# The blockwise inverse of a chunked RWKV-7 scan: two groups of heads in turn, a product on all four 64x64 tiles of TensorE, and other joins

## The reference

```python
def step(S, inp):
    r_t, w_t, k_t, v_t, kk_t, b_t = inp
    sa = jnp.einsum('bhvk,bhk->bhv', S, -kk_t)
    S = (S * w_t[:, :, None, :] + sa[..., None] * b_t[:, :, None, :]
         + v_t[..., None] * k_t[:, :, None, :])
    y_t = jnp.einsum('bhvk,bhk->bhv', S, r_t)
    return S, y_t
```

## Time and profile before

| | us |
|---|---|
| median of 3 runs | 1396.06 |
| lowest, highest | 1393.89, 1396.39 |
| the profiled execution | 1395.23 |
| its span | 1393.4 |
| chunk 0, levels and joins (span time) | 100.5 to 134.1 |
| chunk 1, levels and joins (span time) | 160.5 to 185.4 |

### The profile page before, as it was taken

The page is one execution under the profiler, slowest core; times in us unless marked ns, Lnnn a source line. Parts: engine busy times, 40 slices in busy tenths (PEclk is TensorE's granted clock), DMA queues, the critical chain, the costliest instruction groups (busy, mean ns, idle before and its releaser), DMA issues.

```text
span 1393.4 us, 23529 instructions
## 1 busy us (share of the span) xinstructions
PE 1363.5 (98%) x9838; PEld 1175.4 (84%) x9838; DVE 950.9 (68%) x1480; ACT 748.2 (54%) x1262; POOL 62.7 (5%) x63
## 2 busy tenths in 40 slices
PE   6999999999999999999999999999999999999998
PEld 6789888888889778888899877888888898788886
DVE  7896776766675776756667545576666697767565
ACT  6874435555456575545453446455545536555543
POOL 0003440000010000000000000000000000000000
PEclk9999999999999999999999999999999999999999
DMA  9411016555555315555565553545555553455551
GB/s 333 165 65 33 4 36 238 182 188 193 194 205 173 133 59 169 194 186 199 189 233 182 182 180 123 181 166 197 182 195 194 198 176 127 151 184 194 196 184 58
DMA packets 35290, 230.67 MB, mean 166 GB/s; under 512 B 4176, under 2 KB 5504, under 8 KB 8560
## 3 DMA queue, kind: packets, MB, share of 16 engines
q1 hardware_dynamic: 33376, 223.43, 46.4%
q0 software_dynamic: 1808, 5.74, 1.2%
HBM read 228.08 MB, written 1.05 MB: 164 GB/s over the span
## 4 chain that ended last, share of the span: by engine, by line
PE 91%; DVE 6%; ACT 2%; issue 0%; DMA 0%; SPq 0%; DVEq 0%; ACTq 0%
PE bank L1805 17%; PE bank L1806 17%; PE bank L1807 17%; PE bank L1930 17%; PE bank L1933 8%; PE bank L2197 3%; PE bank L1762 1%; DVE wlo L992 1%; PE bank L2003 1%; PE bank L2021 1%; PE bank L2037 1%; PE bank L2214 1%; PE bank L2375 0%; ACT arena L629 0%; PE bank L2376 0%
## 5 line engine op out<-in xcount | busy, mean ns | idle before, releaser
L992 DVE TENSOR_TENSOR wlo<-raw,whi 128x1024 fp32r<-128x1024 f32 (+1 forms) x416 | 492.9, 1204 | 249.9 <-ACT whi L454 245.5
L454 ACT ACTIVATE whi<-raw 128x1024 fp32r<-128x1024 f32 (+1 forms) x416 | 425.4, 1041 | 329.4 <-PE bank L1807 231.7
L1805 PE MATMUL bank<-whi,XHL 128*128 128x512 f32 x872 | 342.2, 392 | 0.0
L1806 PE MATMUL bank<-wlo,XHL 128*128 128x512 f32 x872 | 339.6, 389 | 0.0
L1807 PE MATMUL bank<-whi,XHL 128*128 128x512 f32 x872 | 339.5, 389 | 0.0
L1930 PE MATMUL bank<-XHL,whi 128*128 128x512 f32 x1008 | 316.6, 395 | 0.2
L1933 PEld LDWEIGHTS bank<-XHL,wlo 128*128 128x128 f32 x1008 | 189.3, 188 | 44.5
L1933 PE MATMUL bank<-XHL,wlo 128*128 128x256 f32 x1008 | 198.0, 278 | 0.0
L1805 PEld LDWEIGHTS bank<-whi,XHL 128*128 128x128 f32 x872 | 163.7, 188 | 34.2 <-issue 1.7
L1807 PEld LDWEIGHTS bank<-whi,XHL 128*128 128x128 f32 x872 | 163.7, 188 | 34.2
L1806 PEld LDWEIGHTS bank<-wlo,XHL 128*128 128x128 f32 x872 | 163.8, 188 | 32.7 <-issue 0.5
(11 more groups left out here) (302 smaller groups left out, 1265.0 us busy)
## 6 DMA issues: line engine op xcount, KB each, us to landing
raw<-in_w_mlp SPq DMA_DIRECT2D x128, 1024.0 KB, 4.9
raw<-in_w_rv SPq DMA_DIRECT2D x8, 1024.0 KB, 4.9
raw<-in_w_rg SPq DMA_DIRECT2D x8, 1024.0 KB, 5.0
raw<-in_w_reo SPq DMA_DIRECT2D x8, 1024.0 KB, 4.9
raw<-in_w_k SPq DMA_DIRECT2D x4, 1024.0 KB, 10.8
raw<-in_w_v SPq DMA_DIRECT2D x4, 1024.0 KB, 10.0
raw<-in_w_r SPq DMA_DIRECT2D x4, 1024.0 KB, 5.0
raw<-in_w_rwo SPq DMA_DIRECT2D x4, 1024.0 KB, 5.0
```

The lines of the kernel that those rows point to most:

```text
L454: act.activation(high, full, ACT.Copy).then_inc(hi_done, 1)
L992: dve.tensor_tensor(low, full, high, ALU.subtract).then_inc(lo_done, 1)
L1805: pe.matmul(out_, xh[xs], wh[ws], start=start, stop=False)
L1806: pe.matmul(out_, xh[xs], wl[ws], start=False, stop=False)
```

## The change

The heads are split in another way: two groups `q` of four columns, each with its even and odd heads. Buffers become `[p, q, f, h, s]`. Per level and group:

- `halves(c, i, q)`: the first product of four even and four odd heads. Even heads stay on the two tiles of before, odd heads write the other half of the partitions (`BLOCKS[blk ^ f]`), so all four tiles are used, in the order (0,0), (1,1), (0,1), (1,0).
- ScalarE copies the even heads (128 partitions, 256 wide) and, in two copies of 64 partitions, puts the odd heads' halves back in place.
- `inverse(c, i, q)`: the second product, as before on two tiles; it waits for the even copy, and then for the odd ones. VectorE subtracts and transposes by group.

The order on TensorE is `halves` of group 0, `inverse` of group 1 of the level before, `halves` of group 1, `inverse` of group 0.

The corner of even and odd heads shares one bank and one copy. The first join is made by group, on two tiles; the second comes behind the first pair products and (in chunk 0) the bonus sum, and the copies' waits move to the `sa` product of the first group. Four bonus products move from level 4 to level 2. `zero_tail` goes: the upper tokens of the `sa` product contract 64 rows instead of 128.

```diff
             def level(c, i, work):
 
-                for f in range(2):
-                    n = 10 * c + 2 * i + f
-                    rows = slice(0, P if i < 4 else HD)
+                rows = slice(0, P if i < 4 else HD)
+                for q in range(2):
+                    n = 10 * c + 2 * i + q
                     dve.wait_ge(inv_prod, n + 1)
-                    dve.tensor_tensor(TI_[rows, f], TI_[rows, f], bank8(6 + f)[rows], ALU.subtract).then_inc(inv_doubled, 1)
-                for f in range(2):
+                    ti = flat(TI_[rows, q])
+                    dve.tensor_tensor(ti, ti, psum[INVERSE_BANK[q]][rows, :], ALU.subtract).then_inc(inv_doubled, 1)
                     if i < 4:
-                        dve.wait_ge(inv_doubled, 10 * c + 2 * i + f + 1)
-                        dve.transpose(TT_[:, f], TI_[:, f]).then_inc(doubled, 1)
+                        dve.wait_ge(inv_doubled, n + 1)
+                        dve.transpose(flat(TT_[:, q]), flat(TI_[:, q])).then_inc(doubled, 1)
...
-                for i in range(5):
-                    for f in range(2):
-                        act.wait_ge(half_prod, 10 * c + 2 * i + f + 1)
-                        act.activation(PM[c][:, f], psum[4 + f][:, :].rearrange("p (h s) -> p h s", h=KT), ACT.Copy)\
-                            .then_inc(half_ready, 1)
+                for i in range(5):
+                    for q in range(2):
+                        even, odd = (psum[b][:, 0:T].rearrange("p (h s) -> p h s", h=4) for b in HALF_BANK[q])
+                        act.wait_ge(half_prod, 10 * c + 2 * i + q + 1)
+                        act.activation(PM[c][:, q, 0], even, ACT.Copy).then_inc(half_ready, 1)
+                        for to, source in ((TOP, LOW), (LOW, TOP)):
+                            act.activation(PM[c][to, q, 1], odd[source], ACT.Copy).then_inc(half_ready, 1)
...
-                if i == 4:
-                    dve.wait_ge(rho_ready, 2)
+                for q in {2: (0,), 4: (1,)}.get(i, ()):
+                    dve.wait_ge(rho_ready, q + 1)
...
-                    for p in range(KT):
+                    for p in range(4 * q, 4 * q + 4):
...
+            def halves(c, i, q):
+
+                keys = MBM[c][i % 2] if i else FIRST_KEYS[c]
+                if i == 0:
+                    pe.wait_ge(ti_ready, 2 * c + 2)
+                    pe.wait_ge(first_masked, 2 * c + 2)
+                    pe.wait_ge(corner_ready, c + 1)
+                    pe.wait_ge(beta_ready, 2 * c + 2)
...
+                else:
+                    pe.wait_ge(inv_doubled, 10 * c + 2 * (i - 1) + q + 1)
+                    pe.wait_ge(level_masked, 8 * c + 2 * (i - 1) + q + 1)
+                for h in range(4):
+                    for f in range(2):
+                        for blk in range(2):
+                            rows, o = BLOCKS[blk], BLOCKS[blk ^ f]
+                            ins = pe.matmul(psum[HALF_BANK[q][f]][o, h * HD:(h + 1) * HD], keys[rows, q, f, h],
+                                            TI_[rows, q, f, h], start=(h == 0), stop=(h == 3))
+                ins.then_inc(half_prod, 1)
+
+            def inverse(c, i, q):
+
+                for f in range(2):
+                    pe.wait_ge(half_ready, 30 * c + 6 * i + 3 * q + 2 * f + 1)
...
+                    ins = both(INVERSE_BANK[q], TT_, PM[c], q, f, 2 if i < 4 else 1)
+                ins.then_inc(inv_prod, 1)
+                if i == 4:
+                    for f in range(2):
+                        ins = both(STEP_BANK[q], PM[c], TT_, q, f)
+                    ins.then_inc(step_prod, 1)
+
+            def first_join(c, q):
+
+                pe.wait_ge(inv_doubled, 10 * c + 8 + q + 1)
+                pe.wait_ge(last_doubled, 2 * c + q + 1)
+                for h in range(4):
+                    p, cols = 4 * q + h, slice(h * HD, (h + 1) * HD)
+                    pe.matmul(psum[JOIN_BANK[q]][LOW, cols], CORNER[TOP, p], TI_[TOP, q, 0, h], start=(h == 0), stop=(h == 3))
+                    ins = pe.matmul(psum[JOIN_BANK[q]][TOP, cols], CORNER[LOW, p], TT_[LOW, q, 1, h], start=(h == 0),
+                                    stop=(h == 3))
+                ins.then_inc(p1_prod, 1)
+
+            def second_join(c):
+
+                pe.wait_ge(p1_ready, 2 * c + 2)
                 for p in range(KT):
...
+                    q, h, cols = p // 4, p % 4, slice(p * HD, (p + 1) * HD)
+                    for f, w, x in ((0, JOIN[LOW, p], TT_[LOW, q, 0, h]), (1, TI_[TOP, q, 1, h], JOIN[TOP, p])):
+                        ins = pe.matmul(psum[6 + f][TOP, cols], w, x, start=(p == 0), stop=(p == KT - 1))
...
                 for i in range(5):
...
+                    halves(c, i, 0)
                     if c == 0 and i < 4:
                         next(r_second)
+                    if i:
+                        inverse(c, i - 1, 1)
+                    halves(c, i, 1)
                     if c == 0 and i == 0:
                         next(r_second)
+                    inverse(c, i, 0)
+                inverse(c, 4, 1)
+                for q in range(2):
+                    first_join(c, q)
...
                 pair_products(c, 0)
...
+                second_join(c)
                 for g in range(4):
...
                     if g == 0:
-                        pe.wait_ge(tail_zeroed, c + 1)
+                        pe.wait_ge(t12_ready, 2 * c + 2)
+                        pe.wait_ge(t22_ready, 2 * c + 2)
                     for h in range(4):
                         p, f = 2 * g + h // 2, h % 2
-                        for t, w in zip(TOKEN_HALVES, (TT_, PM[c])):
-                            ins = pe.matmul(psum[4][t, 256 + h * HD:256 + (h + 1) * HD], w[:, f, p],
-                                            SR[g % 2][:, h * HD:(h + 1) * HD], start=(h == 0), stop=(h == 3))
+                        for t, rows, w in ((TOP, TOP, TT_), (LOW, slice(0, P), PM[c])):
+                            ins = pe.matmul(psum[4][t, 256 + h * HD:256 + (h + 1) * HD], w[rows, p // 4, f, p % 4],
+                                            SR[g % 2][rows, h * HD:(h + 1) * HD], start=(h == 0), stop=(h == 3))
```

More of the change, by code:

```diff
@@ L1714, in _ @@
             pool.wait_ge(gate_ready, 4)
-            zero_tail(1)
             pool.wait_ge(h_lo, 4 * MLP_STEPS)
@@ L2165, in corner @@
                         rows, ts, _ = half_tiles(c, f, 0)
-                        ins = pe.matmul(psum[4 * c + f][0:HD, p * HD:(p + 1) * HD], BE[rows, p, ts], AR[rows, 2 * p + c, 0, HD:P],
+                        be, kap = BE[rows, p, ts], AR[rows, 2 * p + c, 0, HD:P]
+                        ins = pe.matmul(psum[4 * c][rows, p * HD:(p + 1) * HD], kap if f else be, be if f else kap,
                                         start=(p == 0), stop=(p == KT - 1))
-                        if p == KT - 1:
-                            ins.then_inc(corner_prod, 1)
+                ins.then_inc(corner_prod, 1)
             def r_tiles():
@@ L2191, in _, with both @@
                 next(r_second)
-            def both(bank, w, x, f, blocks=2):
-                for p in range(KT):
-                    for blk in range(blocks):
-                        rows = slice(blk * HD, (blk + 1) * HD)
-                        ins = pe.matmul(psum[bank][rows, p * HD:(p + 1) * HD], w[rows, f, p], x[rows, f, p],
-                                        start=(p == 0), stop=(p == KT - 1))
-                return ins
+            BLOCKS = (TOP, LOW)
+            def both(bank, w, x, q, f, blocks=2):
+                for h in range(4):
+                    for blk in range(blocks):
+                        rows = BLOCKS[blk]
+                        ins = pe.matmul(psum[bank][rows, f * T + h * HD:f * T + (h + 1) * HD], w[rows, q, f, h],
+                                        x[rows, q, f, h], start=(h == 0 and f == 0), stop=(h == 3 and f == 1))
+                return ins
@@ L2244, in _ @@
                     if c == 0 and i < 4:
                         next(r_second)
-                    for f in range(2):
-                        n = 10 * c + 2 * i + f
-                        pe.wait_ge(half_ready, n + 1)
-                        if c and i == 0 and f == 0:
-                            pe.wait_ge(keys_ready, 4)
-                            pe.wait_ge(state_ready, 8)
-                        if i:
-                            pe.wait_ge(doubled, n - 1)
-                        else:
-                            pe.wait_ge(tt_ready, 2 * c + f + 1)
-                        both(6 + f, TT_, PM[c], f, 2 if i < 4 else 1).then_inc(inv_prod, 1)
-                        if i == 4:
-                            both(f, PM[c], TT_, f).then_inc(step_prod, 1)
+                    if i:
+                        inverse(c, i - 1, 1)
@@ L2314, in _ @@
                             pe.wait_ge(keys_ready, g)
+                        else:
+                            pe.wait_ge(t12_ready, 2)
                         for s, src in enumerate((BE, kT)):
@@ L2330, in _ @@
```

(2 more changed lines are left out.)

135 lines of the change are left out of this document (60 added, 75 removed).

## The result

The changed kernel takes 1413.18 us (1411.59 to 1413.69) against 1394.97 us for the kernel before, a ratio of 1.0129 with a 95% interval of 1.0117 to 1.0142. It is slower, as forecast. The forecast of 1410 was 3 us low: 1413.18 lies 0.2 us above its own range (1407 to 1413) and inside the wider one (1399.5 to 1416). The medians lie 18.2 us apart, where 14.5 was added up. The profiled execution took 1411.59 us with a span of 1409.8, that is 16.4 us more than the one of before, at the full granted clock (0.999 over the whole span); it was the fastest of the four, and the other three took 1.3 to 2.1 us more at granted clocks of 0.996 to 0.998.

What follows compares the result with a forecast made beforehand. TensorE, busy for 98% of the span, was taken as the bound. Terms 1.6 + 0.2 + 3.1 + 9.6 = 14.5 us gave 1410 us, own range 1407 to 1413, eight in ten 1399.5 to 1416.

Steps and rivals of the forecast that it cites:

- The gap: TensorE's wait for VectorE's subtraction between a group's second and next first product: priced at 1.0 us, about 0.8 shown idle.
- H: First product of an inverse level, 32 instructions per head group: on four tiles 0.51 us instead of 0.96.
- three pieces of the price: Wait at each half level: last matmul's start to VectorE 0.27, subtraction 0.69, VectorE's end to weight load 0.05; together 1.0 us.
- Chunk 0: First chunk's inverse, with a projection tile inside five levels that covers nothing: +3.1 us up to the bonus turn.
- Chunk 1: Second chunk's inverse and joins to the second pair products: +1.6 us, and +0.2 for VectorE's normalisation.
- H0(0): Group 0's first product at level 0 of the inverse, the zero from which chunk 1's times were counted.
- H0(1): Group 0's first product at level 1, put at 3.2 us in chunk 1, with the three copies overlapping.
- The mixed product: Product with the inverse, alternating 64-row and 128-row matmuls, eight times: seven shape changes, 1.2 us each product, +9.6 us.
- the upper bound: Mixed product's dearer end: each first weight load exposed by 0.05 us more, +1.4 us a product, 11.2 in all.
- No drain between the shapes: Rival for the mixed product: alternating shapes cost nothing, only the inverse's 4.9 us remain, 1401.0 us; chance 0.18.
- A stagger that hides its own subtraction: Rival for the inverse's order: no product waits for its own group's subtraction, 1386 us; chance 0.06.
- A dearer drain: Rival for the mixed product: each shape change waits 0.22 plus 0.05 us, 2.2 a product, 17.5 in all, 1418; chance 0.06.

Runs made afterwards that it cites:

- e3: Changed kernel with both groups' first products, then the projection tile, then both groups' second products on TensorE: 1400.46 us, ratio 1.0035 to the kernel before.
- e1: Changed kernel with the product with the inverse contracting 128 rows for both token halves again, GpSimd clearing the lower half: 1401.79 us against 1395.85, ratio 1.0043.
- e2: Kernel before with one edit alone, upper tokens of the product with the inverse contracting 64 rows instead of 128: 1405.46 us, ratio 1.0068.
- e6: Changed kernel with uniform 128-row product, both groups' first products ahead of both second products, and odd heads' first product on the even heads' two tiles: 1396.33 us.
- e11: Changed kernel with uniform product, first products ahead of second, projection tile between first products, GpSimd's clearing ahead of its last gating: 1392.34 us against 1395.65, ratio 0.9977.
- e12: As e11, but ScalarE reads the second projection tile behind level 4's copies, not ahead of them: 1390.74 us against 1394.27 for the kernel before, ratio 0.9965.

## Why the prediction was right, step by step

**The gap.** The idle time was put at about 0.8 us; it is 0.79 at most half levels, and sixteen waits make 13.6 us. Half a level was put at 2.44 us and took 2.41, H at 0.51 and took 0.52 (176.01 to 176.53), and the subtractions of one group lie 4.81 apart (175.27 to 180.08) where 4.9 was said. The sum of the three pieces of the price, all read from the kernel before, held. e3 shows the cause: with the same four tiles, copies and joins, another order alone takes off 10.65 us. That is more than the 4.9 us that the inverse was charged, since it also collects what the four tiles save.

**Chunk 0.** Forecast +3.1 to the bonus turn; measured 48.60 - 45.41 = +3.19. One of its terms can be seen by itself: the bonus products at level 2 were charged 0.4, and the gap that they lengthen is 1.28 instead of 0.79, so 0.49. VectorE, then TensorE, in chunk 0:

```profile
127.03 1.63 DVE L1430 SCALAR_TENSOR_TENSOR raw<-arena,vecs 128x256 f32<-128x256 f32 x4
129.32 0.69 PE L2225 MATMUL bank<-arena 64*64 64x64 f32 x32 [1.28 <-DVE arena L1359]
```

**Chunk 1.** Forecast +1.8 from H0(0) to the second pair products; measured 200.87 - 170.14 = 30.73 against 28.41, so +2.3. The total is nearer than its terms, since some of their errors cancel. H0(1) came 3.47 us after H0(0), not 3.2: the three copies do not overlap and end 1.94 us after H0(0), the 1.95 that was passed over for 1.75. The seven half levels behind it, at 2.41 instead of 2.44, gave 0.25 back. The normalisation on VectorE lengthened two of their gaps, to 0.86 (at 183.29) and to 1.15 (the row below), 0.43 us in all where 0.2 was charged:

```profile
188.47 0.69 PE L2225 MATMUL bank<-arena 64*64 64x64 f32 x32 [1.15 <-DVE arena L1359]
```

Behind the joins, the join and the carried rows took 0.29 less than reckoned and the right-hand sides 0.54 more. That last is the term of chunk 1 that was most mis-sized, and the step that was missed in it is VectorE's work beside GpSimd. Timeline of GpSimd, VectorE and TensorE behind the joins, which answers to the earlier trace rows:

```profile
196.61 1.27 POOL L1700 TENSOR_TENSOR arena<-arena 128x512 f32<-128x512 f32 x1
```
```profile
196.65 1.78 DVE L1402 SCALAR_TENSOR_TENSOR arena<-small,arena 128x512 f32<-128x512 f32 x1
198.35 2.19 DVE L1380 TENSOR_TENSOR arena<-bank,c_pair_masks 64x192 f32<-64x192 f32 x8
```
```profile
196.78 0.70 PE L2279 MATMUL bank<-arena 64*128 64x256 f32 x4
200.60 0.34 PE L2336 MATMUL bank<-arena 128*64 128x64 f32 x4 [0.20 <-DVE arena L1380]
200.87 0.70 PE L2279 MATMUL bank<-arena 64*128 64x256 f32 x4
```

The last normalisation piece (L1402) takes 1.78 us here and 0.69 in this kernel's three records where GpSimd has nothing to do (at 162.44, 212.88 and 225.58), so the masks (L1380) begin only at 198.35 and the right-hand sides wait for them: 1.02 us from 199.85 to 200.87, where 0.48 was reckoned. In the kernel before, the same piece (L1392, 1.22 us from 183.51) was over when the masks fell due at 186.43. The forecast counted VectorE's free time per half level but not what is left over behind the last one. No run took GpSimd's work away from there, so this account rests on the records alone.

**The mixed product.** Forecast +1.2 each and +9.6 in all, bounds 8.4 to 11.2; measured 1.91 - 0.51 = +1.40 each (8 x 1.40 = 11.2), and 11.3 in the scan by e1 and by e2. The mechanism was right, and the size is that of the upper bound, +1.4, where I took 1.2 from between the bounds; +1.7 us in all. The rows at 145.18 and 145.44 show why: the change takes the 0.15 of the earlier trace rows, and within a matmul the second instruction comes 0.11 after the first instead of 0.059, which is the 0.05 more that the upper bound allowed for. With the 0.5 of chunk 1 and the 0.1 of chunk 0 this makes 2.3, and the scan grew by 16.86 where 14.5 were forecast. Behind the scan the profiled execution of after was 1.2 us shorter (1187.5 against 1188.7), and its scan began 0.8 later, which gives the 16.4 of the spans.

**The rivals.** No drain between the shapes (1401) falls with e2: the edit alone costs 9.6 us (1405.46 - 1395.85). A stagger that hides its own subtraction (1386) falls with the sixteen gaps. A dearer drain (17.5 us) falls with 11.3; its own price of 0.27 a change gives 7 x 0.27 = 1.9 us a product and 15 us in all, not 2.2 and 17.5, and that too is above the measured 1.40. The two costs are independent: the inverse's order 10.65 and the mixed product 11.29 add up to 21.94, of which 20.87 come back together, and the rest is a named wait for GpSimd.

## What to carry to other kernels

When each step of a chain needs a short operation of another engine, the queue order decides whether that operation is free. Write down what stands directly ahead of the dependent product: if it is the product whose result the other engine must first finish, the round trip is exposed at every step, however much work the step has lost. Keep matmuls of one tile shape together, since an alternation is no idle time in a profile but a longer busy group; and when a faster order is found, look for the next engine that was only just in time (here ScalarE's copies, its reading of a projection, GpSimd's clearing).

## What was not expected of the hardware

- A change between 64-row and 128-row tiles cost 0.20 us, with the lost work side by side in it, even though the two shapes used different column halves: 1.91 against 0.51 us over seven changes.
- VectorE's 128x512 operations with both operands outside the banks took up to 1.78 us beside GpSimd's (L1402) instead of 0.69 (its three records without GpSimd at work), while the subtraction, with one operand in a bank, stayed at 0.69 (L1359). The Trainium skill (GPSIMD Engine Reference, Specifications) names this contention for VectorE's instructions with two SBUF inputs; 1.78 against 0.69 agrees.
- ScalarE's copies of 64 partitions into the other half cost nearly what copies in place cost: 0.78 for two (L786, e3) against 0.77 in e6. The three of a group, from the first start to the last end, take 1.19 (167.82 to 169.01 in e3) against 1.05 in place (166.17 to 167.22 in e6).
- In e11 the granted clock was 0.50 from about 127.1 to about 130.5, behind a stretch with 2.23 busy us of TensorE in 3.60 and idle pieces of 0.57 and 0.85. The group of 91 took 5.65 us there and 3.72 at full clock. The changed kernel, with 13.6 us of idle time in sixteen pieces, kept 1.00 throughout the scan. What tells the two apart was not settled; e12, which removed the 0.85, kept the full clock.
